# Rotary partner rows by transfers within SBUF, and rotations half a chunk later

## The reference

```python
h = rms_norm(x, g_pre_mix[l])
proj = h @ w_in[l]
mq, mk, mv, rq, rk, rv, rg = jnp.split(proj, SPLIT_POINTS, axis=-1)
mq = rotary(split_heads(mq, MOBA_HEADS), moba_inv, ROPE_DIM)
mk = rotary(split_heads(mk, MOBA_HEADS), moba_inv, ROPE_DIM)
mo = merge_heads(moba_attention(mq, mk, split_heads(mv, MOBA_HEADS)))
rq = rotary(split_heads(rq, RET_HEADS), ret_inv, RET_QK_DIM)
rk = rotary(split_heads(rk, RET_HEADS), ret_inv, RET_QK_DIM) * (RET_QK_DIM ** -0.5)
ro = retention(rq, rk, split_heads(rv, RET_HEADS))
```

## Time and profile before

| what | value |
|---|---|
| time, median of 3 runs | 1481.89 us (1479.58 to 1482.81) |
| time of the profiled execution | 1478.86 us |
| its span | 1477.0 us |
| PE busy | 1452.9 us, 98% of the span |
| DVE busy | 828.9 us, 56% |
| ACT busy | 687.7 us, 47% |
| GpSimd busy | 43.2 us, 3% |
| granted TensorE clock | 0.995 of full speed in the mean |
| stage of the rotations | 1038 to 1130 us of the span |

### The profile page before, as it was taken

How to read it: one execution, slowest core, us unless ns; L and a number is a source line. 1 busy time by engine, 2 the same in 40 slices (tenths; PEclk the granted TensorE clock), 3 DMA queues, 4 the chain that set the end, 5 groups by cost and what they waited for, 6 DMA issues and landing times.

```text
span 1477.0 us, 18731 instructions
## 1 busy us (share of the span) xinstructions
PE 1452.9 (98%) x7412; PEld 1224.2 (83%) x7412; DVE 828.9 (56%) x927; ACT 687.7 (47%) x899; POOL 43.2 (3%) x96
## 2 busy tenths in 40 slices
PE   8999999999999999999999999999999999899997
PEld 6888889988888888888888788888787989788886
DVE  5655565865454555455666464554865565554454
ACT  6545445454444544435445455444544444544442
POOL 1000000000000000000000000000100100000000
PEclk9999999999999999999999999999999999999999
DMA  9755554445555455554444346455433543255551
GB/s 356 260 193 189 181 177 166 171 154 213 178 196 190 152 203 196 189 184 169 171 143 143 114 173 254 174 197 180 176 115 114 189 168 143 100 199 199 181 191 57
DMA packets 38574, 262.14 MB, mean 177 GB/s; under 512 B 4288, under 2 KB 4544, under 8 KB 7648
## 3 DMA queue, kind: packets, MB, share of 16 engines
q1 hardware_dynamic: 37152, 252.85, 48.4%
q0 software_dynamic: 1344, 8.16, 1.4%
HBM read 259.95 MB, written 1.05 MB: 177 GB/s over the span
## 4 chain that ended last, share of the span: by engine, by line
PE 95%; ACT 1%; DVE 1%; SPq 1%; DMA 1%; issue 0%; POOL 0%; POOLq 0%; DVEq 0%; ACTq 0%
PE prod L1001 15%; PE prod L1003 15%; PE prod L1002 15%; PE acc L1001 9%; PE acc L1003 9%; PE acc L1002 9%; PE prod L995 4%; PE prod L996 4%; PE prod L997 4%; PE acc L1168 2%; PE aux L1031 2%; PE acc L1018 1%; DMA raw<-in_weights_dram 1%; PE acc L1187 1%; PE o_bank L1220 1%; ACT acts_h L1319 0%
## 5 line engine op out<-in xcount | busy, mean ns | idle before, releaser
L1489 DVE TENSOR_TENSOR w_lo<-raw,w_hi 128x2048 fp32r<-128x2048 f32 x235 | 538.2, 2291 | 341.3 <-ACT w_hi L1301 341.1
L1301 ACT CAST w_hi<-raw 128x2048 fp32r<-128x2048 f32 x235 | 448.0, 1907 | 293.6 <-PE acc L1003 177.3
L1001 PE MATMUL prod<-w_hi,acts_h 128*128 128x512 f32 x944 | 375.9, 398 | 2.5 <-DVE w_lo L1497 1.7
L1003 PE MATMUL prod<-w_hi,acts_l 128*128 128x512 f32 x944 | 368.8, 391 | 0.0
L1002 PE MATMUL prod<-w_lo,acts_h 128*128 128x512 f32 x944 | 368.4, 390 | 0.0
L1001 PE MATMUL acc<-w_hi,mix_h 128*128 128x512 f32 x600 | 236.7, 395 | 0.3 <-DVE small L1581 0.3
L1003 PE MATMUL acc<-w_hi,mix_l 128*128 128x512 f32 x600 | 233.8, 390 | 0.0
L1002 PE MATMUL acc<-w_lo,mix_h 128*128 128x512 f32 x600 | 233.5, 389 | 0.0
L1001 PEld LDWEIGHTS prod<-w_hi,acts_h 128*128 128x128 f32 x944 | 177.8, 188 | 42.9 <-issue 7.0
L1003 PEld LDWEIGHTS prod<-w_hi,acts_l 128*128 128x128 f32 x944 | 177.5, 188 | 37.7
L1002 PEld LDWEIGHTS prod<-w_lo,acts_h 128*128 128x128 f32 x944 | 177.9, 188 | 35.1 <-issue 0.5
(11 more groups left out here) (255 smaller groups left out, 1220.9 us busy)
## 6 DMA issues: line engine op xcount, KB each, us to landing
raw<-in_weights_dram SPq DMA_DIRECT2D x235, 1024.0 KB, 4.9
raw<-in_weights_dram SPq DMA_DIRECT2D x12, 256.0 KB, 6.6
work<-in_mem_dram POOLq DMA_DIRECT2D x2, 1024.0 KB, 13.4
grow<-in_gain_rows_dram POOLq DMA_DIRECT2D x4, 512.0 KB, 4.4
tabs<-in_tabs_dram POOLq DMA_DIRECT2D x1, 1696.0 KB, 9.4
work<-in_x_t_dram SPq DMA_DIRECT2D x4, 256.0 KB, 6.3
x_res<-in_x_dram SPq DMA_DIRECT2D x1, 1024.0 KB, 8.7
work<-in_mem_t_dram POOLq DMA_DIRECT2D x1, 1024.0 KB, 14.4
```

The lines of the kernel that those rows point to most:

```text
L1001: pe.matmul(out, still_hi, wh, start=first, stop=False, skip_group_check=True)
L1003: return pe.matmul(out, still_lo, wh, start=False, stop=last, skip_group_check=True)
L1301: act.copy(w_hi[:, c % RING], raw[:, c % RAW]).then_inc(hi_done, 1)
L1489: dve.tensor_tensor(w_lo[:, c % RING], raw[:, c % RAW], w_hi[:, c % RING].bitcast(F32), ALU.subtract).then_inc(lo_done, 1)
```

## The change

The permutation matmul goes. In its place GpSimd issues four transfers within SBUF for each rotation: for each of the two heads in a tile, the upper half of the rotary rows goes to the place of the lower in `rotated`, and the lower to that of the upper. They move 8 partitions each for q0, k0, q2 and k2, and 32 each for rq and rk, with 2 KB for each partition. Before the first, GpSimd fills `rotated` with zeros; before each later one it waits until the rotation before is done, since there is one buffer `rotated`. DVE waits for the four transfers (`halves_moved`) and not for `aux_done`, and multiplies `rotated` in place. The sine table takes the sign, and the two permutation tables go.

The rotations of q2, k2, rq and rk move from the middle of the next chunk to its end, behind that chunk's own read and ahead of the tick there; `ready` is called ahead of that tick, with the counts that hold then.

```diff
     def rope(self, dest, at, which, read):
-        self.add("rope", dest=dest, at=at, which=which, read=read, aux=self.aux)
-        self.aux += 1
         self.rope_n += 1
+        self.add("rope", dest=dest, at=at, which=which, read=read, n=self.rope_n)
...
-    def roped_slot(dest, at, which, read, units=()):
-        def go():
-            pl.rope(dest, at, which, read)
-            slot()
-            pl.ready(units)
-        return go
+    def roped_end(dest, at, which, read, units=()):
+
+        pl.rope(dest, at, which, read)
+        pl.ready(units)
+        end(slot)
...
-    pl.project(w, 512 + COLS, "k", 2, mid=roped_slot("q", 2, "moba", pl.read))
-    end(slot)
-    pl.project(w, 1536, "k", 4, mid=roped_slot("k", 2, "moba", pl.read, moba[4:8]))
-    end(slot)
-    pl.project(w, 1792, "k", 6, mid=roped_slot("k", 4, "ret", pl.read))
-    end(slot)
+    q_read = pl.read
+    pl.project(w, 512 + COLS, "k", 2, mid=slot)
+    roped_end("q", 2, "moba", q_read)
+    k_read = pl.read
+    pl.project(w, 1536, "k", 4, mid=slot)
+    roped_end("k", 2, "moba", k_read, moba[4:8])
+    rq_read = pl.read
+    pl.project(w, 1792, "k", 6, mid=slot)
+    roped_end("k", 4, "ret", rq_read)
     rk_read = pl.read
-    mids = [roped_slot("k", 6, "ret", rk_read, ret), slot]
-    pl.project_tokens(w, 2048, "v", 512, mid=lambda: mids.pop(0)(), between=lambda: end(slot))
+    pl.project_tokens(w, 2048, "v", 512, mid=slot, between=lambda: roped_end("k", 6, "ret", rk_read, ret))
...
+                elif kind == "rope":
+                    if it["n"] == 1:
+                        own(pool.memset(rotated, 0.0))
+                    else:
+                        pool.wait_ge(roped, it["n"] - 1)
+                    pool.wait_ge(prod_read, it["read"])
+                    half = ROPE_HALF[it["which"]]
+                    for base in (0, 64):
+                        for to, of in ((base, base + half), (base + half, base)):
+                            pool.dma_start(rotated[to:to + half], dests[it["dest"]][of:of + half, it["at"]:it["at"] + 2]
+                                           ).then_inc(halves_moved, 16)
...
-                elif kind == "rope":
-                    pe.wait_ge(prod_read, it["read"])
-                    reader(pe, it["aux_reader"])
-                    pe.matmul(aux[:], table("perm_" + it["which"]),
-                              dests[it["dest"]][:, it["at"]:it["at"] + 2, :].rearrange("p a b -> p (a b)"),
-                              start=True, stop=True).then_inc(aux_done, 1)
...
                 elif kind == "rope":
-                    dve.wait_ge(aux_done, it["aux"] + 1)
+                    dve.wait_ge(halves_moved, 64 * it["n"])
                     t = dests[it["dest"]][:, it["at"]:it["at"] + 2]
-                    rot = rotated
-                    own(dve.tensor_tensor(rot, aux[:].rearrange("p (a b) -> p a b", a=2),
-                                          bcast(table("sin_" + it["which"]), 2), ALU.mult))
+                    own(dve.tensor_tensor(rotated, rotated, bcast(table("sin_" + it["which"]), 2), ALU.mult))
                     own(dve.tensor_tensor(t, t, bcast(table("cos_" + it["which"]), 2), ALU.mult))
-                    dve.tensor_tensor(t, t, rot, ALU.add).then_inc(roped, 1)
+                    dve.tensor_tensor(t, t, rotated, ALU.add).then_inc(roped, 1)
```

More of the change, by code:

```diff
@@ L54 @@
 _at = 0
-for _name, _width in (("ident", P), ("perm_moba", P), ("perm_ret", P), ("alibi", S),
-                      ("mask", S), ("cos_moba", S), ("sin_moba", S), ("cos_ret", S),
+for _name, _width in (("ident", P), ("alibi", S), ("mask", S), ("cos_moba", S), ("sin_moba", S), ("cos_ret", S),
                       ("sin_ret", S), ("inv_count", 4 * 16), ("decay", 4 * 384)):
@@ L60 @@
 N_TABLES = _at
-FIRST_TABLES = TABLES["perm_moba"][0]
+FIRST_TABLES = TABLES["alibi"][0]
+ROPE_HALF = {"moba": 8, "ret": 32}
 def tables():
@@ L79, in tables @@
     pos = np.arange(S, dtype=np.float64)[None, :]
[L81 to L85, removed]
+    for name, inv in (("moba", 500000.0 ** (-np.arange(8) * 2.0 / 16)),
+                      ("ret", 1.0 / 10000.0 ** np.linspace(0.0, 1.0, 32))):
+        half = ROPE_HALF[name]
         cos, sin = np.ones((P, S)), np.zeros((P, S))
@@ L89, in tables @@
                 a, b = base + i, base + half + i
-                perm[b, a] = -1.0
-                perm[a, b] = 1.0
-                for r in (a, b):
+                for r, sign in ((a, -1.0), (b, 1.0)):
                     cos[r] = np.cos(pos * inv[i])
-                    sin[r] = np.sin(pos * inv[i])
-        put("perm_" + name, perm)
+                    sin[r] = sign * np.sin(pos * inv[i])
         put("cos_" + name, cos)
@@ L837, in build @@
         roped = sem("roped")
+        halves_moved = sem("halves_moved")
         pooled = sem("pooled")
@@ L1796, in number @@
     turned_heads = None
-    n = dict(acc_turned=0, decay=0, rope=0, max=0, turned=0, o_hi=0, outs=0, mix_hi=0, mixed=0, half=0, row=0,
+    n = dict(acc_turned=0, decay=0, max=0, turned=0, o_hi=0, outs=0, mix_hi=0, mixed=0, half=0, row=0,
              squared=0, scaled=0)
@@ L1847, in number @@
             it["aux_reader"], aux_reader = aux_reader, ("mid_lo", it["m"] + 1)
-        elif kind == "rope":
-            n["rope"] += 1
-            it["aux_reader"], aux_reader = aux_reader, ("roped", n["rope"])
         elif kind == "second_squares":
```

## The result

| | median us | lowest to highest | runs |
|---|---|---|---|
| before | 1479.99 | 1477.80 to 1482.81 | 21 |
| changed | 1481.82 | 1479.24 to 1486.50 | 21 |

The ratio is 1.0018, with an interval of 1.0011 to 1.0026. The change costs 1.8 us in the median. In the mean it costs 2.7 (1482.61 against 1479.89), because the changed kernel's runs spread upwards further. It is slower, as I had forecast, but by 0.18%, where I had given 0.70 to slower by over 0.2%. One execution of the kernel before, beside the first experiments, took 3757.86 us and is left out of every ratio here.

What follows compares the result with a forecast made beforehand. PE was taken to bound the kernel, busy 98% of the span and 95% of the chain. Queue terms +1.4 and clock +2.6 made +4.0 us on the median 1481.89: 1485.9, rounded to 1486; range 1482.5 to 1492.

Steps and rivals of the forecast that it cites:

- queue terms: Changes to PE's queue in the stage of the rotations: +0.9 - 0.86 + 2.15 - 0.86 + 0.1 = +1.4 us.
- the clock: Behind PE's two new waits of about 3 us, low clock costs 1.3 us each: +2.6 us.
- q0 and k0: At the first scores: k0's set must wait for q0's rotation (one buffer), so PE scores later: +0.9 us.
- rk: At the first retention scores: PE waits 0.95 us for rk's rotation, less 0.86 for the product gone: +0.1 us.
- q2: q2's rotation, moved to its chunk's end, just fits on DVE; PE saves the product: -0.86 us.
- k2: End of rq's chunk, head 4's scores: PE idles 3.0 us for k2's rotation, less 0.86 saved: +2.15 us.
- rq: Nobody asks for rq's rotation at its own tick, so PE saves the product: -0.86 us.
- the milder form of the last rival: The later slow stretch at 1203 is not met any more: 1.7 us less than the sums; no separate chance.
- not slower: Rival: clock keeps its level through both new waits, sets land in 1.8 us: +1.0 us, 1482.9; chance 0.25.
- The late sets: Rival: DVE's splits and passes hold back q0's and k0's transfers: sum +8.8, with the clock 1494 us; chance 0.15.
- The gain of 5.2 us: Rival: no new wait arises, PE keeps the six products of 0.86 us saved: 1476.7 us; chance 0.05.
- The signs to look for: In the profile after: PE waits at head 4's, first and first retention scores; DVE idle before k0's rotation; low clock.

Runs made afterwards that it cites:

- the version with eight: The changed kernel with each set of four transfers issued twice, first into columns nobody reads then: 1506.23 us, ratio 1.0181 against before.
- the one with five: The changed kernel with one more transfer, first in each set, into columns nobody reads then: 1491.05 us, ratio 1.0077 against before.

## Why the prediction missed, step by step

The miss of 4.2 us (1486.0 against 1481.82) is made up of 1.9 from the base, 1.1 from the queue terms and 1.1 from the clock (taken as what is left of 1.8 without the queue's 0.3). Against the right base the change was forecast at +4.0 and measured at +1.8, so the terms of q0 and k0, of rk and of the clock were sized too high, and that is the step that failed in the prediction of the change itself.

**The base.** I added +4.0 to 1481.89, the median of three runs. The median of 21 is 1479.99; the three lay 1.9 us too high, by chance. I had seen that the profiled execution was 3.0 below their median, and chose the median. This step alone accounts for nearly half of the miss of 4.2 us. On 1480.0 the same sum and the same margins would have given 1484.0 and a range from 1480.6, which holds the time.

**The queue terms.** Their sum was +1.4; the trace has +0.3 to +0.4.

| term | forecast | measured |
|---|---|---|
| q0 and k0 | +0.9 | +0.40 |
| q2 | -0.86 | -0.86 |
| k2 | +2.15 | +2.09 |
| rq | -0.86 | -0.86 |
| rk | +0.1 | -0.41 |

The step that speaks against the change, k2, was right in place, mechanism and size, and the run with that one rotation back bears it out: the queue is 2.9 us shorter. Mis-sized were two. For q0 and k0 a set was taken at 0.54 us an issue and 2.2 of landing; it is 0.50 and 1.8, so k0's rotation came 0.5 us earlier than forecast (1062.5 on before's time, not 1063.0). For rk I gave PE a wait of 0.95; it is 0.45 in the changed kernel and 0.43 in two others, since DVE's chain of splits, masks and rotation is that much shorter than my sum of rows.

**The clock.** +2.6 was forecast as twice 1.3. The profiled execution of the changed kernel shows no fall behind the first wait and one behind the second, at half the full clock:

```profile
1070.00:1080.00 10.00, 10.00 (x77) 9.07 (x76) 6.99 (x17) 5.14 (x14) 1.98 (x4) 1.00 0.45 162
...
1097.90:1101.30 3.40, 3.40 (x13) 2.68 (x14) 3.35 (x8) 1.25 (x5) 1.29 (x3) 0.51 0.34 77
```

In the mean of the runs the term was right: 2.7 us of loss less 0.3 of queue leave 2.4. In the median only 1.5 is left. The fall happens in some executions and not in others, and the unlucky ones pull the mean. I forecast a median with a term that was a mean. That the mean came within 0.2 us of 2.6 is partly luck, since 1.3 was a middle between nothing and 3.3.

**Not used.** In the profiled execution the low stretch at 1203 of before is missing, as the milder form of the last rival had it. It is no gain of the change: the wait of 1.8 us there is followed by a low clock in 3 of the 11 profiled executions of this study, and in 8 not.

**The rivals.** What came is nearest to "not slower" (sum +1.0, within 0.2%). Its landing of 1.8 us and its first term of +0.5 were right (1.8 and +0.40), its main reason was not: the clock did not keep its level. The late sets are refuted as I had drawn them: k0's four issues ran beside DVE's split of 1059.05 (1059.42 to 1061.39, the split until 1061.33) and took 0.49 us each. By the rule of the Trainium skill (GPSIMD Engine Reference, the section with the table of SBUF interfaces), GpSimd and VectorE contend for SBUF when VectorE's instruction has two inputs there, as the split has; for the issue of transfers this trace shows nothing of it. Yet the result of that rival, 1494, is what one transfer more gave (1491), by another mechanism that I had not on my list: by all that the packets show, the weights' tiles. The gain of 5.2 us came in no version; the best of the queues is -3.3.

**The signs to look for.** Of the five, four were there: the wait of 3 us at head 4's scores, the wait of 3 at the first scores, an idle DVE ahead of k0's rotation (1.3, I had said 1.6) and none at q2's and k2's, and a low clock behind one wait. The wait at the first retention scores was half of what I said.

## What to carry to other kernels

When a step is moved later to give a transfer time, look for the first user behind the new place and count what stands between: here the transfer needed 3.2 us and had most of a chunk either way, while k2's rotation, moved behind the chunk's read, made PE wait for three passes. A small transfer on another queue should be planned against the large ones in flight: whether it gets its packets out before the next tile of weights decided 2.5 to 3.4 us a set here, and a change that fits by 0.2 us is one edit away from losing 9. And add a forecast to a median of many runs, not of three, when the effect is a quarter of a per cent.

## What the runs showed of the hardware

**Transfers within SBUF from GpSimd's queue.** 16 KB and 64 KB alike: 0.50 us an issue, 1.7 to 2.1 us to landing when nothing large is in flight, and up to 5.5 us (in the version with eight; 5.0 in the one with five) when a tile of 1 MB is.

**Whether the clock falls behind a short wait differs from execution to execution.** In the 11 profiled executions the wait of 4.0 us late in the kernel was followed by a low clock every time, for 6.8 to 10.2 us. The waits of 2.3 to 3.1 us in this stage were followed by one 5 times out of 8, for 3.4 or 6.8 us. The wait of 2.1 us at the kernel's start (2.2 and 2.4 in two of them), code that no version changes, 4 times out of 11, and the wait of 1.8 us near 1200, 3 times out of 11. The loss over the eight waits of 2.3 to 3.1 us is 10 us, or 1.25 for each.

**Idle work may pay.** Three products that nobody reads, in a wait of 3 us, shortened the kernel by 1.2 to 1.5 us in the three pairs with and without them (1481.8 to 1480.6, 1478.4 to 1477.0, 1477.0 to 1475.5), with a queue that was at most 0.2 longer. In the first pair the intervals of the ratios only touch (at 1.0011), in the other two they overlap; all three go the same way. The second buffer gained 1.4 and 1.5 us in its two pairs, with intervals that overlap too, and the traces account for 0.3 to 0.4 of it; where the rest comes from, or whether it is chance, is open.
